# Differential attention stretch: score masks one step earlier, low parts one step later, two powers for one, four modulation pieces in the FFN

## What is computed

```python
x = x + swiglu(h, e_ffn_gate, e_ffn_up, e_ffn_down)          # even layer's FFN
q, k, v = split(rms_norm(x) @ w_qkv)                         # 8 heads, 2 halves of 64
q = partial_rope(rms_norm(q, q_norm)); k = partial_rope(rms_norm(k, k_norm))
s = einsum(q_blk, k) * 64 ** -0.5                            # per head h, half c, 128 queries
s = where(kpos <= qpos, s, -inf); p = softmax(s)
attn = p[:, :, 0] - lam * p[:, :, 1]
o = rms_norm(attn @ v, subln) * (1 - lambda_init); x = x + o @ w_o
```

## Time and profile before

| what | us |
|---|---|
| median of 3 runs | 2155.21 |
| the profiled execution's own time | 2152.07 |
| its span, first to last instruction | 2150.3 |
| DVE busy / PE busy / ACT busy / POOL busy, whole span | 1565.6 / 1919.5 / 1180.2 / 108.5 |
| stretch from the first product of the queries (549.4) to the last of w_o (739.3) | 189.8 |

### The profile page before, as it was taken

How to read it: one execution, slowest core, us unless ns; L and a number is a source line. 1 busy time by engine, 2 the same in 40 slices (tenths; PEclk the granted TensorE clock), 3 DMA queues, 4 the chain that set the end, 5 groups by cost and what they waited for, 6 DMA issues and landing times. The chain is left out here.

```text
span 2150.3 us, 25644 instructions
## 1 busy us (share of the span) xinstructions
PE 1919.5 (89%) x9324; PEld 1611.4 (75%) x9324; DVE 1565.6 (73%) x1478; ACT 1180.2 (55%) x1263; POOL 108.5 (5%) x103
## 2 busy tenths in 40 slices
PE   8749978999965799999999999999999989678957
PEld 8648867788844678888888888888888878467746
DVE  6687355887847479988888898888888975446544
ACT  5411214343435456766677667667766754565364
POOL 1000000111011000000000000000000000310040
PEclk9868659999976899999999999999999999679958
DMA  7300005898622379999999999999999945104410
GB/s 254 111 1 1 30 20 176 302 318 282 221 70 69 128 265 378 336 372 347 367 345 362 374 341 372 335 379 344 365 351 354 381 137 179 59 20 149 140 41 20
DMA packets 161947, 489.01 MB, mean 227 GB/s; under 512 B 8177, under 2 KB 13425, under 8 KB 161744
## 3 DMA queue, kind: packets, MB, share of 16 engines
q1 hardware_dynamic: 153536, 458.21, 58.7%
q0 software_dynamic: 8336, 29.81, 3.9%
HBM read 485.36 MB, written 2.62 MB: 227 GB/s over the span
## 5 line engine op out<-in xcount | busy, mean ns | idle before, releaser
L2410 DVE TENSOR_TENSOR expert_weights_low<-BIG,expert_weights_high 128x2048 fp32r<-128x2048 f32 x336 | 750.4, 2287 | 57.3 <-ACT expert_weights_high L2970 57.1
L2970 ACT ACTIVATE expert_weights_high<-BIG 128x2048 fp32r<-128x2048 f32 x336 | 625.9, 1922 | 67.9 <-DMA BIG<-in_o_moe_up 42.5
L1151 PE MATMUL bank<-expert_weights_high,expert_x_high 128*128 128x512 f32 x896 | 352.0, 393 | 2.4 <-DVE expert_x_low L2475 2.3
L1153 PE MATMUL bank<-expert_weights_low,expert_x_high 128*128 128x512 f32 x896 | 349.7, 390 | 0.0
L1152 PE MATMUL bank<-expert_weights_high,expert_x_low 128*128 128x512 f32 x896 | 349.5, 390 | 0.0
L1812 DVE TENSOR_TENSOR weights_at<-BIG,weights_at 128x2048 fp32r<-128x2048 f32 (+2 forms) x100 | 219.7, 2197 | 134.4 <-ACT weights_at L2656 132.9
L2656 ACT ACTIVATE weights_at<-BIG 128x2048 fp32r<-128x2048 f32 (+2 forms) x100 | 183.5, 1835 | 200.9 <-DMA BIG<-in_e_ffn_gate 34.2
L1151 PE MATMUL bank<-weights_at,x_high 128*128 128x512 f32 (+2 forms) x608 | 244.0, 401 | 22.4 <-DVE x_low L1839 11.0
L1152 PE MATMUL bank<-weights_at,x_low 128*128 128x512 f32 (+2 forms) x608 | 239.5, 394 | 0.0
L1153 PE MATMUL bank<-weights_at,x_high 128*128 128x512 f32 (+2 forms) x608 | 239.1, 393 | 0.0
L1151 PEld LDWEIGHTS bank<-expert_weights_high,expert_x_high 128*128 128x128 f32 x896 | 168.7, 188 | 37.0 <-DVE expert_x_low L2475 2.4
(11 more groups left out here) (400 smaller groups left out, 2475.4 us busy)
## 6 DMA issues: line engine op xcount, KB each, us to landing
BIG<-in_o_moe_gate SPq DMA_DIRECT2D x112, 1024.0 KB, 5.1
BIG<-in_o_moe_up SPq DMA_DIRECT2D x112, 1024.0 KB, 5.3
BIG<-in_o_moe_down SPq DMA_DIRECT2D x112, 1024.0 KB, 5.3
BIG<-in_w_ada POOLq DMA_DIRECT2D x48, 512.0 KB, 4.8
BIG<-in_w_in SPq DMA_DIRECT2D x20, 1024.0 KB, 5.0
BIG<-in_o_w_qkv SPq DMA_DIRECT2D x12, 1024.0 KB, 5.1
BIG<-in_e_w_in SPq DMA_DIRECT2D x10, 1024.0 KB, 5.8
BIG<-in_e_ffn_gate SPq DMA_DIRECT2D x10, 1024.0 KB, 5.1
```

Of the source, the lines that this page charges most:

```text
L1151: mm(b, high_l, high_r, start=start, stop=False, skip_group_check=not check)
L1153: last = mm(b, high_l, low_r, start=False, stop=stop, skip_group_check=not check)
L2410: tt_(E_WL[q % E_SLOTS], half(q % E_SLOTS), E_WH[q % E_SLOTS].bitcast(F32), SUB).then_inc(w_low, 1)
L2970: f(E_WH[q % E_SLOTS], half(q % E_SLOTS), ACT.Copy).then_inc(w_high, 1)
```

## The change

Edits in four places, none of them to what is computed.

1. FFN: the last `ada(1)` of a chunk becomes `ada(2)` for c = 2 to 5, so that all 24 pieces are done there; the two `ada(2)` between the query tiles go.
2. Powers: POOL raises 16 sums (queries) and 16 sums (keys) by themselves; `scaled` waits for the second. The rotation is a function `turned(hf, q)` of its own: queries are turned right behind their sums, keys behind their scaling. Its temporaries move to another place.
3. DVE masks step i + 1 ahead of the weights of step i, in both halves; its low parts come one step after ACT's high parts. ACT's second head squares move from i = 5 behind the step to the start of i = 6.
4. PE computes the scores of i + 2 ahead of the unit of an iteration, in place of behind it (`outputs` is what is left of `step`: transposes of i, values of i - 1); unit 10 comes behind `heads_to_channels(1)`, unit 11 behind the scores of 8 and 9.

```diff
@@ make_plan and the PE stream (same order in both)
-            for i in range(9):
-                qkv_unit(i + 2)
-                step(i, 8)
-            qkv_unit(11)
+            for i in range(8):
+                if i < 6:
+                    scores(i + 2)
+                qkv_unit(i + 2)
+                outputs(i, 8)
+            outputs(8, 8)
             heads_to_channels(1)
+            qkv_unit(10)
             scores(8)
             scores(9)
+            qkv_unit(11)
             for i in range(8, 17):
+                if i < 14:
+                    scores(i + 2)
@@ POOL
-            def diff_root(hf):
-                pool.wait_ge(diff_sums, hf + 1)
-                a = s_qk[:, 32 * hf:32 * hf + 32]
+            def diff_root(hf, q):
+                n = 2 * hf + q
+                pool.wait_ge(diff_sums, n + 1)
+                a = s_qk[:, 16 * n:16 * n + 16]
@@ DVE, FFN
-                    ada(1)
+                    ada(1 if c == 1 else 2)
@@ DVE, rotation
+            def turned(hf, q):
+                x = QKVB[:, :, q * D + hf * BANK:q * D + (hf + 1) * BANK].rearrange("p m (g w) -> p m g w", w=64)
...
+                for i, a in enumerate((x1, x2, x2, x1)):
+                    V(tt_(t[i], a, bc(ROPE[:, q, :, i, :], 2, [P, TT, 8, 8]), MUL))
+                V(tt_(x1, t[0], t[1], SUB))
+                V(tt_(x2, t[2], t[3], ADD), diff_ready if q else None)
@@ DVE, attention stretch
             low_to(tile(5))
-            ada(2)
             sums(0, 0)
+            turned(0, 0)
             low_to(tile(6))
             qkv_out(2)
-            ada(2)
             low_to(tile(7))
             sums(0, 1)
             low_to(tile(8))
             scaled(0)
+            turned(0, 1)
             qkv_out(4)
...
-            for i in range(9):
-                if i < 8:
-                    weighted(i)
-                if i + 1 < 8:
+            for i in range(8):
+                if i < 7:
                     masked(i + 1)
+                weighted(i)
+                if i % 2:
+                    low_to(tile(9 + i // 2))
...
+            scaled(1)
+            turned(1, 1)
             heads_out(1)
             masked(8)
+            low_to(tile(13))
+            qkv_out(QKV_ORDER[5])
+            o_sums_of(0)
             for i in range(8, 16):
+                if i < 15:
+                    masked(i + 1)
                 weighted(i)
@@ ACT, attention stretch
-            for i in range(9):
-                if i + 1 < 8:
+            for i in range(8):
+                if i == 6:
+                    head_squares(1, 1)
+                if i < 7:
                     exponentials(i + 1)
+                if i % 2 == 0:
+                    high_to(tile(9 + i // 2))
...
+            values_out(7)
             high_to(tile(13))
             heads_out(1)
+            qkv_out(QKV_ORDER[5])
             exponentials(8)
```

More of the change, by code:

```diff
@@ L269, in scores, with outputs @@
             add(("diff", "scores", i, c), "e", 2 + 2 * (i % 2) + c)
-    def step(i, end, first=0):
-        if i + 2 < end:
-            scores(i + 2)
+    def outputs(i, end, first=0):
         if i < end:
@@ L290, in make_plan @@
             chunk(c, m)
[L291 to L292 removed]
+        outputs(i, 8)
+    outputs(8, 8)
     for u in range(4, 8):
         add(("qkT", u), "av"[u % 2], u - 2)
+    chunk(QKV_ORDER[5], 0)
     scores(8)
     scores(9)
+    chunk(QKV_ORDER[5], 1)
     for i in range(8, 17):
+        if i < 14:
+            scores(i + 2)
         if i == 10:
@@ L300, in make_plan @@
                 add(("oT", u), "v", u)
-        step(i, 16, 8)
+        outputs(i, 16, 8)
     for u in range(2):
@@ L1092, in _ @@
             pool.wait_ge(filled, PLAN.filled(("Up", 0, 1)))
-            modulation_weights(0, ADA_FFN + ADA_SLOTS)
+            modulation_weights(0, ADA * KD)
             inverse_root(2)
-            modulation_weights(ADA_FFN + ADA_SLOTS, ADA * KD)
-            diff_root(0)
-            diff_root(1)
+            for hf in range(2):
+                diff_root(hf, 0)
+                diff_root(hf, 1)
             pool.wait_ge(diff_ready, 2)
@@ L2373, in _ @@
                 elif i == 11:
+                    low_to(tile(14))
+                elif i == 12:
                     low_to(tile(15))
@@ L2923, in _ @@
                     qkv_out(c)
-                if i % 2 == 0 and i < 6:
-                    high_to(tile(9 + i // 2))
-                if i < 8:
-                    weights_out(i)
+                weights_out(i)
                 if i:
```

47 lines of the change are left out of this document (13 added, 34 removed).

## The result

The changed kernel takes 2133.43 us (median of 4 runs, 2131.26 to 2140.52) against 2154.24 us for the kernel before (4 runs, 2152.07 to 2155.56): a ratio of 0.991, interval 0.9884 to 0.9936. It is faster by some 20 us; the forecast was 2135 (its sum gives 2135.7). The profiled execution took 2131.26 us with a span of 2129.3, 21.0 us less than the span of before.

What follows compares the result with a forecast made beforehand. PE bounds the FFN; from 592 us on neither PE nor DVE does, they wait for each other. +2.5 - 12.2 - 7.8 - 2.0 = -19.5 gives 2132.6, as a median 2135.7, rounded to 2135; range 2121 to 2148 us.

Steps and rivals of the forecast that it cites:

- The FFN: Four more modulation pieces in the FFN delay the queries: +2.5 us, 2.35 of it the piece of chunk 5.
- The stall before the heads: Query, key and value stage: all 10.98 us of PE's wait go, unit 1 starts 12.2 us sooner.
- the low clock would go with the idle: At the first heads: 16 transposes at full clock take 2.3 us instead of 3.67.
- rule of the Trainium skill: DVE and GpSimd block each other fully on their shared port; by it the sum would lose 2 us.
- The first half: Steps 0 to 7, unit 1 to the transposes of step 8: -7.8 us, ends -21 and 0.
- my three streams: First-half steps followed on PE, DVE and ACT side by side: values of 7 at 44 us from unit 1's start.
- The second half: Steps from 8 on, to the last unit of w_o: -2.0 us, between +2 and -6.
- waits for line 2310 under 5 us: Sign: PE's waits for weights, 14.4 us in the profile before, fall under 5 us.
- Scores ahead of the unit: Rival, first-half steps: scores of i + 2 block PE for exponentials every step; +8, 2163 us; chance 0.06.
- PE becomes the bound: Rival, first half: all waits for weights go, second heads in time, -19 for -7.8; 2124 us; chance 0.15.
- Only the stall goes: Rival: only the wait before the first heads goes, the attention's gain is eaten; -9.7, 2145.5 us; chance 0.13.
- The FFN pays in full: Rival, FFN: the four added pieces cost 9.4 us for 2.5; 2142 us; chance 0.06.

Runs made afterwards that it cites:

- variant 1: Changed kernel with the four modulation pieces back between the query tiles, step order and split powers kept: 2138.63 us, ratio 0.9942.
- variant 9: Variant 8 with the modulation piece of the FFN's last chunk moved behind the copy of the first query tile: 2124.07 us, ratio 0.9859.
- Variant 8: Changed kernel with unit 2 ahead of scores 2, unit 1 ahead of the first heads, the modulation's third reduction behind unit 2: 2127.93 us.
- variant 3: Changed kernel with the old order of the steps on PE, DVE and ACT; pieces, powers and turns as changed: 2142.90 us, ratio 0.9956.
- variant 4: Changed kernel with DVE's low parts of tiles 9 to 12 back in the step of ACT's high part, masks still first: 2142.89 us.
- variant 5: Changed kernel with DVE's weights of i ahead of the masks of i + 1 again in the first half: 2134.86 us, ratio 0.9911.
- Variant 12: Variant 6 plus last chunk's piece behind first query copy, masks 9/weights 8 early, high part 14 late, low tile 13 and o's norm later: 2121.77 us.
- variant 6: Changed kernel with unit 2 ahead of the scores of 2 on PE, in step 0 alone: 2130.07 us, ratio 0.9911.
- variant 7: Changed kernel with PE's scores of i + 2 behind the unit in all of the first half: 2129.26 us, ratio 0.9892.
- variant 2: Changed kernel with one power of 32 columns for queries and keys, behind the keys' sums: 2136.02 us, ratio 0.9937.

## Why the prediction was right, and where its steps were not

*The FFN.* Forecast +2.5, measured +2.2 to the queries, and +2.4 from the first product of the FFN's last tile to them. Variants 1 and 9 show that it is the piece of chunk 5 and no other: without it the gap is 7.06 and 7.07 us. From the first gate product of chunk 1 to the first product of its last tile it took 187.24 us after and 187.45 before, so the three other pieces cost nothing that shows.

*The stall before the heads.* The total was right (-11.8 for -12.2), its make-up less so. PE reached the heads 0.8 us sooner than the old times plus 2.5 us gave (41.58 us behind the queries for 42.37). Against that, the transposes took 3.65 us and not 2.3, and unit 1 came 4.61 us behind their start (3.4 in the forecast). I had put the low clock of the earlier trace rows down to the 10.98 us of idle, and let it go with them. PE was never idle ahead of 593.18, and still the stretch behind it has the low clock (PEclk is the third number from the end; 0.50 is the lower level, 1.2 GHz):

```profile
580.00:589.00 9.00, 9.00 (x41) 7.29 (x40) 5.35 (x4) 3.97 (x4) 2.90 (x1) 1.00 0.72 236
589.00:593.20 4.20, 4.20 (x35) 4.16 (x33) 3.93 (x9) 0.00 (x0) 0.00 (x0) 0.86 0.57 168
593.20:597.00 3.80, 3.63 (x17) 3.23 (x17) 1.42 (x4) 1.37 (x2) 0.00 (x0) 0.50 0.23 90
```

What PE did in the second of these is the 32 one-column matmuls of line 1431, and the clock fell within them. Variant 8 puts the heads ahead of them and the heads run in 1.97 us; the low clock then comes behind the reduction in its new place. So the step of the forecast that failed here is that the low clock would go with the idle: in this place it needs none. Idle is not thereby cleared: behind the 3.49 us at 607.21 unit 2 ran at 0.63 us a product, and behind the 2.14 us at 639.08 unit 9 did. In the kernel before, reduction and idle both lay ahead of the heads, and no run parts them there.

*The powers.* Three of 2.90 and one of 3.01 us, forecast 2.9 with up to 5 for the keys; no key power fell behind a low part here, but in variant 1 it did (5.01). The rule of the Trainium skill that I weighed (SBUF — State Buffer, SBUF: two separate sides) held in one direction only, in these runs too: POOL's power waits for a product with two SBUF inputs already under way, but the low part at 576.65 and the four turns from 574.68 on (the first of them 0.05 us ahead of the power, three inside it) ran beside the power of 574.73 at their usual 2.29 and 1.27 us. The 2 us which the page's rule would have cost did not come.

*The first half.* -8.2 for -7.8, in part by luck. Unit 1 and the scores of 0 and 1 took 5.9 us for 3.9, as unit 1 had the low clock, which the forecast had gone by then. The wait for the first exponentials was 3.49 us (forecast 3.4), the one behind step 5 2.14 (2). PE's idle before the second heads was 0.91, not 4, since the eight steps ended later than my three streams had it (the last values at 47.9 us behind unit 1, not 44); the heads were ready at 49.5 us behind unit 1 against 47 to 49, and the rest (13.96 us to step 8) was 2 us shorter than forecast, so that the sum came within half a microsecond. Several of its terms were off by 2 to 4 us and cancelled. The part that was shown apart is the size of the order: 8.6 us (variant 3); taken out of it, the late low part costs 11.3 (variant 4) and the early masks 3.6 (variant 5).

*The second half.* -0.7 for -2.0, and "waits for line 2310 under 5 us" was wrong: 12.2 us are left, in both halves. PE's waits from step 8 to the gates, before (679 to 717.2 us) and after (661 to 699 us):

```profile
PE bank L1151 <- DVE x_low L1839: 5.8, 1, 5.8
PE bank L1522 <- ACT BIG L2904: 2.5, 1, 2.5
PE bank L1513 <- ACTq L2889: 2.4, 1, 2.4
PE bank L1522 <- DVE BIG L2310: 1.4, 2, 1.0
```
```profile
PE bank L1526 <- DVE BIG L2320: 10.0, 4, 3.3
PE bank L1155 <- DVE x_low L1847: 1.9, 1, 1.9
PE bank L1517 <- ACTq L2899: 1.0, 2, 0.6
```

Both lists count the wait that ends as the stretch begins: 0.33 us at 679.04 and 3.34 us at 661.25, which lie in the stretch ahead. Without them 11.6 us of waiting became 9.6: the one wait of 5.8 for a low part was cut to 1.9, the one of 2.5 for ACT is gone, and three steps now wait for their weights, 2.08, 2.73 and 1.86 us. Of these 2 us only 0.7 arrive at the gates; PE was busy for longer there (27.71 us for 26.35, with about the same instructions), since more of its products took 0.63 us. I had counted the masks' new place and ACT's high part, but not that DVE brings copy, low part and normalization into steps which only two units cover. Variant 12 moves just these, and the high part, and the stretch is 2.1 us shorter than in the kernel after (35.28).

*The rivals.* "Scores ahead of the unit" had the mechanism right for the first step and wrong for the others: the exponentials of later steps held PE up by 0.8 us at most, as the forecast held. What it costs is the first wait with the clock behind it, 3.9 us (variant 6), or 2.9 with all scores behind their units (variant 7). "PE becomes the bound" would have needed all the waits for weights gone and unit 1 to step 8 in 52.7 us. In the kernel after 12.2 of the 14.4 us of these waits are left, and in no variant did that stretch fall below 55.95 us; that variant 12 takes 2121.8 us, near this rival's 2124, comes from its other stretches too. "Only the stall goes" is in effect variant 3: 2142.9 us where that rival gave 2145.5. "The FFN pays in full" is excluded by 2.4 us.

## What to carry to other kernels

When engines take turns in a loop, an in-order queue should hold nothing whose producer runs in the same step: moving one 2.3 us operation a step behind its producer gained 11.3 us over eight steps once the rest was reordered, and the rest does not pay without it (2.7 us lost against the old order); from the old order, with the new streams of PE and ACT, it gained 5.0. Look for free slots by the gap behind the instruction that waits, and price the new neighbour: a small operation on POOL started right behind a large one on DVE lost 2.1 us each time. After a stall is gone, read what is late next in the adjoining stretch, where the same work, moved, may refill the waits one for one.

## What the runs showed of the hardware that I had not expected

- The granted clock fell to 0.50 in and behind a stretch in which PE was busy without a gap, 4.2 us with 32 one-column matmuls, and the 16 transposes behind it took 3.65 us instead of 1.97. How long it stays low differs: unit 1 ran mostly low in the kernel after (0.63 us a product) and at 1.00 in variant 6, with the same work ahead of it. The two earlier reductions, in the FFN, have 512-column products at 0.63 us behind them too (528.6 to 533.4 us in the kernel after), though not in every trace: in variant 2 the one at 524.26 is followed by products at 0.39 and a granted clock of 1.00.
- A power on POOL costs by its columns, on 128 partitions: 0.71 us for 2, 1.65 for 8, 2.90 for 16, 5.43 for 32. Started within 0.1 us behind a DVE product of 2.29 us with two SBUF inputs it takes 2.1 more (3.75 for 8, 5.01 for 16, 7.56 for 32), and behind a shorter one less: 1.0 more for the 2 columns below, which start 0.04 us behind the first of two such products of 1024 columns (line 2397 of the kernel before, 2.48 us for the two). The product that starts while the power runs takes no longer.

```profile
743.35 1.74 POOL L1037 TENSOR_TENSOR SM<-SM 128x2 f32<-128x2 f32 x1 [23.32 <-DVE SM L1794]
```

- The kernel after and the variants 2 to 8, whose code up to the queries is the same, reach the queries between 549.2 and 555.8 us. A gain of 2 us in a stretch was plain in the trace and not in four or five times.
